# Mixing input projections as three products of rounded parts, their weights split in nine pieces

## What is computed

```python
def token_mix(x, w_in, w_out, ...):
    h = x @ w_in                       # (256, 1024) @ (1024, 2344)
    (nq, kc, vc, ks, vs, kw, vw, gl, u, gq, gk, gv, ga, gr) = jnp.split(h, split_pts, axis=-1)
    gates = jax.nn.sigmoid(gl).reshape(B, S, NSA_HEADS, 3)
    o_a = nsa_mixer(nq, kv(kc), kv(vc), kv(ks), kv(vs), kv(kw), kv(vw), gates, ...)
    o_b = pool_mixer(u, pool_w, pool_scale)
    o_c = gla_mixer(gq, gk, gv, ga, gr, gla_wa2, gla_ba, gla_norm_g)
    return jnp.concatenate([o_a, o_b, o_c], axis=-1) @ w_out
```

## Time and profile before

| what | value |
|---|---|
| time, median of three runs (lowest, highest) | 2362.57 us (2362.32, 2368.52) |
| time of the profiled execution | 2365.88 us |
| its span, first to last instruction | 2364.1 us |
| granted TensorE clock, mean | 0.990 |
| busy: TensorE / weight loads / VectorE / ScalarE / GpSimd | 98% / 81% / 76% / 55% / 7% |
| input projections of mix0, first to last | 201.78 to 263.59 us |

### The profile page before, as it was taken

How to read it: one execution, slowest core, us unless ns; L and a number is a source line. 1 busy time by engine, 2 the same in 40 slices (tenths; PEclk the granted TensorE clock), 3 DMA queues, 4 the chain that set the end, 5 groups by cost and what they waited for, 6 DMA issues and landing times.

```text
span 2364.1 us, 32857 instructions
## 1 busy us (share of the span) xinstructions
PE 2306.4 (98%) x12939; PEld 1907.8 (81%) x12939; DVE 1791.7 (76%) x2006; ACT 1290.6 (55%) x1374; POOL 173.6 (7%) x211
## 2 busy tenths in 40 slices
PE   9999999999999999999999998999999999999997
PEld 7888878878888788889877886678888888888875
DVE  6873468767862678778585568869998989889988
ACT  4432444434432644444544447657777777778774
POOL 1100001000100001000010005400000000000010
PEclk9999999999999999999999998999999999999998
DMA  9766258758655266754135543158999999999994
GB/s 376 268 236 199 90 165 306 265 199 299 244 202 181 108 249 249 268 181 148 72 151 197 190 157 117 73 212 345 382 382 376 379 372 384 385 359 388 382 372 192
DMA packets 116613, 596.88 MB, mean 252 GB/s; under 512 B 29000, under 2 KB 29838, under 8 KB 58638
## 3 DMA queue, kind: packets, MB, share of 16 engines
q1 hardware_dynamic: 95764, 521.10, 57.6%
q0 software_dynamic: 20304, 73.98, 9.2%
q10 hardware_dynamic: 428, 0.15, 0.0%
HBM read 589.38 MB, written 5.78 MB: 252 GB/s over the span
## 4 chain that ended last, share of the span: by engine, by line
PE 90%; DVE 5%; ACT 2%; issue 1%; DMA 1%; ACTq 0%; POOL 0%; DVEq 0%; SPq 0%
PE psum L985 19%; PE psum L986 19%; PE psum L1018 13%; PE psum L1135 6%; PE psum L1564 3%; PE psum L1034 3%; PE psum L1571 3%; PE psum L1152 2%; PE psum L3233 2%; PE psum L978 1%; PE psum L979 1%; PE psum L980 1%; PE psum L2320 1%; PE psum L2323 1%; PE psum L2321 1%; DVE ring_r L1238 1%
## 5 line engine op out<-in xcount | busy, mean ns | idle before, releaser
L1238 DVE TENSOR_TENSOR ring_r<-ring,ring_r 128x2048 fp32r<-128x2048 f32 x286 | 652.3, 2287 | 177.2 <-ACT ring_r L1232 176.9
L1232 ACT CAST ring_r<-ring 128x2048 fp32r<-128x2048 f32 x286 | 546.7, 1913 | 380.0 <-PE psum L1018 206.2
L1238 DVE TENSOR_TENSOR ring_r<-ring,tail_r 128x2048 fp32r<-128x2048 f32 x143 | 327.2, 2288 | 91.6 <-ACT tail_r L1232 91.3
L1232 ACT CAST tail_r<-ring 128x2048 fp32r<-128x2048 f32 x143 | 273.3, 1911 | 141.0 <-PE psum L1018 69.3
L985 PE MATMUL psum<-ring_r,arena_r 128*128 128x512 f32 (+1 forms) x872 | 334.6, 387 | 2.8 <-DVE arena_r L1325 2.8
L986 PE MATMUL psum<-ring_r,arena_r 128*128 128x512 f32 (+1 forms) x872 | 330.9, 382 | 0.0
L985 PE MATMUL psum<-ring_r,xT_r 128*128 128x512 f32 (+1 forms) x576 | 215.7, 380 | 2.9 <-ACT ring_r L1232 2.9
L986 PE MATMUL psum<-ring_r,z_r 128*128 128x512 f32 (+1 forms) x576 | 212.6, 375 | 0.0
L1018 PE MATMUL psum<-ring_r,z_r 128*128 128x512 f32 (+1 forms) x864 | 194.8, 369 | 0.0
L985 PEld LDWEIGHTS psum<-ring_r,arena_r 128*128 128x128 f32 x872 | 164.0, 188 | 34.5 <-DVE arena_r L1325 4.0
L986 PEld LDWEIGHTS psum<-ring_r,arena_r 128*128 128x128 f32 x872 | 164.2, 188 | 30.6
(11 more groups left out here) (582 smaller groups left out, 3737.4 us busy)
## 6 DMA issues: line engine op xcount, KB each, us to landing
ring<-in_expert_halves SPq DMA_DIRECT2D x264, 1024.0 KB, 6.7
ring<-in_dense_halves SPq DMA_DIRECT2D x165, 1024.0 KB, 6.9
arena<-in_ada_w POOLq DMA_DIRECT2D x48, 1024.0 KB, 9.4
ring<-in_mlstm_w_in SPq DMA_DIRECT2D x8, 2048.0 KB, 8.4
ring<-in_mix_in SPq DMA_DIRECT2D x4, 2048.0 KB, 8.7
ring<-in_mix_out SPq DMA_DIRECT2D x4, 2048.0 KB, 7.9
ring<-in_glu_panels SPq DMA_DIRECT2D x4, 2048.0 KB, 9.2
ring<-in_mlstm_w_out SPq DMA_DIRECT2D x3, 2048.0 KB, 13.5
```

The source lines that it names most:

```text
L1232: act.copy(upper[i % UPPERS], place(PN[r.key, i])).then_inc(upper_ready, 1)
L1238: dve.tensor_tensor(low, raw, upper[i % UPPERS], ALU.subtract).then_inc(lower_ready, 1)
```

## The change

Both parts of the input projections are now rounded numbers, as in the feed-forward layers. x is split: `copy_xT_act` writes `xh`, `split_xT_dve` writes the low part to `xT_r` (for tile 0 between the statistics and the centering of tile 1). The weights come in nine pieces of 256 to 280 columns (`IN_PIECES`, ga and gr together are "gr", ks and kw "kskw", vs, vw and gl "vsvw"), each with a semaphore of its own. `in_high_act` copies a piece to its rounded part, `in_low_dve` leaves the low part in place. The parts of gv and gr lie in `ada_w`, and so do later those of vsvw, kskw and kcvc; those of gqk, q01, q23 and u lie in slot 3 and tail. gv and gr are asked for before the preceding feed-forward layer's last three halves are done, and ScalarE and VectorE split them ahead of the layer norm. `features` and `tokens` make 24 calls for 8. w1 is loaded behind kcvc, since slot 3 is taken. gr of tile 1 goes to PSUM bank 7 in place of bank 3; bank 7 is where the second pair of q features goes, which therefore waits for sr. vs, vw and gl tokens are one product of 280 columns into banks 0 and 1, so the attention's first product waits for the gates. The buffers pT and p_sb move into `ada_w` too.

```diff
 
-IN_PANELS = [(1560, 512), (2072, 272), (0, 512), (512, 384), (896, 408), (1304, 256)]
-PANEL_END = ("gv", "gr", "q1", "kcvc", "vwgl", "u")
-Q_PANEL = 2
+IN_PIECES = {"gv": [(1816, 256)], "gr": [(2072, 272)], "gqk": [(1560, 256)], "q01": [(0, 256)], "q23": [(256, 256)],
+             "kskw": [(768, 128), (1024, 128)], "vsvw": [(896, 128), (1152, 128), (1280, 24)], "kcvc": [(512, 256)],
+             "u": [(1304, 256)]}
+IN_WIDTH = {name: sum(n for _, n in cols) for name, cols in IN_PIECES.items()}
+IN_AT = {"gv": 0, "gr": 2048, "gqk": 4224, "q01": 6272, "q23": 8320, "kskw": 0, "u": 2048, "vsvw": 4224, "kcvc": 6464}
+IN_END = {"gv": "gv", "gr": "gr", "gqk": "gqk", "q01": "q0", "q23": "q1", "kskw": "kskw", "vsvw": "vwgl", "kcvc": "kcvc", "u": "u"}
+IN_AFTER = {"kskw": ("gv",), "u": ("gr",), "vsvw": ("q0",), "kcvc": ("q1",)}
 
 ML_INNER, ML_HEADS, ML_CONV, QKV_BLOCK = 2 * D, 4, 4, 4
 ML_HD = ML_INNER // ML_HEADS
@@ -346,7 +350,7 @@
 
...
-            for i in range(len(IN_PANELS)):
-                if i == 3:
-                    PN["mix", l, "w1"] = rg.take(3, dmas=GROUPS, over=mixP.after("cmp0", l))
-                PN["mix", l, "in", i] = rg.take(i % 3, over=mixP.after(PANEL_END[i], l))
+            for name, at in IN_AT.items():
+                places = range(at // HALF, -(-(at + KD * IN_WIDTH[name]) // HALF))
+                PN["mix", l, "in", name] = [mixP.after(e, l) for e in IN_AFTER[name]] if name in IN_AFTER else \
+                    [rg.over[place // 2][place % 2] for place in places]
+            rg.over[0] = [mixP.after("kskw", l), mixP.after("u", l)]
+            rg.over[1] = [mixP.after("vwgl", l), mixP.after("kcvc", l)]
+            rg.over[2] = [mixP.after("kcvc", l), mixP.after("q1", l)]
+            rg.over[3] = [mixP.after("gqk", l), mixP.after("q0", l)]
+            PN["mix", l, "w1"] = rg.take(3, dmas=GROUPS, over=mixP.after("cmp0", l))
...
-            dst = xh[:, t, 4 * b:4 * b + 4, :] if q in FFN_OF else \
+            dst = xh[:, t, 4 * b:4 * b + 4, :] if q in FFN_OF or q in MIX_OF else \
...
-                              xh[:, t, part[0], :], ALU.subtract).then_inc(xl_ready, 1)
+                              xh[:, t, part[0], :], ALU.subtract).then_inc(xl_ready if q in FFN_OF else mix_x_low, 1)
...
+    cv = Carve(ada_w_end - 2 * HALF)
+    pT = cv.take(2, 2 * CHUNK)
+    p_sb = cv.take(2, 2 * CHUNK)
+    cv = Carve(ada_w_end - 2 * HALF, of=arena_r)
+    in_high = {name: cv.take(KD * IN_WIDTH["vsvw"]) for name in ("gr", "gv")}
+    in_high.update(vsvw=in_high["gr"], kskw=in_high["gv"], kcvc=in_high["gv"], gqk=upper[0], q01=upper[1], q23=upper[2], u=upper[2])
...
+    def in_place(name, of=None):
+
+        at, n = IN_AT[name], KD * IN_WIDTH[name]
+        return (ring if of is None else of)[:, :, :].rearrange("p s n -> p (s n)")[:, at:at + n]
+
+    def in_parts(name):
+
+        w = IN_WIDTH[name]
+        return [v[:, 0:KD * w].rearrange("p (k w) -> p k w", w=w) for v in (in_high[name], in_place(name, ring_r))]
+
+    def in_high_act(act, l, name):
+
+        act.wait_ge(in_landed[name], 16 * (l + 1))
+        n = (0, 2)[l]
+        if name in ("gv", "gr"):
+            act.wait_ge(ada_ready, 2 * (n + 1) * NC)
+        elif name in ("gqk", "q01", "q23"):
+            act.wait_ge(halves_used, (n + 1) * FFN_HALVES - 2 + ("gqk", "q01", "q23").index(name))
+        else:
+            act.wait_ge(*mixP.after({"kskw": "gv", "vsvw": "gr", "kcvc": "kskw", "u": "q1"}[name], l))
+        act.copy(in_high[name][:, 0:KD * IN_WIDTH[name]], in_place(name)).then_inc(*inH.inc(name, l))
+
+    def in_low_dve(dve, l, name):
+
+        dve.wait_ge(*inH.after(name, l))
+        dve.tensor_tensor(in_place(name, ring_r), in_place(name), in_high[name][:, 0:KD * IN_WIDTH[name]], ALU.subtract)\
+           .then_inc(*inL.inc(name, l))
+
     def mix_sp(sp, l):
-        for i, (_, n) in enumerate(IN_PANELS):
-            if i == 3:
-                pn = PN["mix", l, "w1"]
-                load_panel(sp, pn, [(slot_of(pn)[d * HD:(d + 1) * HD, :], A["mix_compress"][l]) for d in range(GROUPS)])
-            pn = PN["mix", l, "in", i]
-            load_panel(sp, pn, [(slot_of(pn)[:, 0:KD * n], A[f"mix_in{i}"][l])])
+        for name in ("gv", "gr", "gqk", "q01", "q23", "kskw", "u", "vsvw", "kcvc"):
+            for freed, n in PN["mix", l, "in", name]:
+                sp.wait_ge(freed, n)
+            sp.dma_start(in_place(name), A["mix_in_" + name][l]).then_inc(in_landed[name], 16)
+        pn = PN["mix", l, "w1"]
+        load_panel(sp, pn, [(slot_of(pn)[d * HD:(d + 1) * HD, :], A["mix_compress"][l]) for d in range(GROUPS)])
...
-        return bank(5 - 2 * t)[:, 0:16 + GLA_H * GLA_V]
+        return bank(5 + 2 * t)[:, 0:16 + GLA_H * GLA_V]
 
     def mix_pe(pe, l, q):
-        def features(dst, i, first, m):
-            w = IN_PANELS[i][1]
-            pe.wait_ge(*landed(pn[i]))
+        def features(dst, name, first, m):
+            high, low = in_parts(name)
+            dst = dst.rearrange("p (t n) -> p t n", t=NT)
+            parts = ((xh, high, inH), (xh, low, inL), (None, high, inL))
+            for i, (of, w, ready) in enumerate(parts):
+                pe.wait_ge(*ready.after(name, l))
+                for k in range(KD):
+                    moved = of[:, :, k, :] if of is not None else xT_r[:, k, :].rearrange("p (t n) -> p t n", t=NT)
+                    mm = pe.matmul(dst, w[:, k, first:first + m], moved, start=i == 0 and k == 0, stop=i == 2 and k == KD - 1)
+            return mm
+
+        def tokens(dst, name, t, between=None):
+            high, low = in_parts(name)
+            pe.wait_ge(*inH.after(name, l))
             for k in range(KD):
-                mm = pe.matmul(dst, panel(pn[i], KD, w)[:, k, first:first + m], xT[:, k, :], start=k == 0, stop=k == KD - 1)
-            return mm
-
-        def tokens(dst, i, first, m, t):
-            w = IN_PANELS[i][1]
-            pe.wait_ge(*landed(pn[i]))
+                pe.matmul(dst, xh[:, t, k, :], high[:, k, :], start=k == 0, stop=False)
+            pe.wait_ge(*inL.after(name, l))
             for k in range(KD):
-                mm = pe.matmul(dst, xT[:, k, t * P:(t + 1) * P], panel(pn[i], KD, w)[:, k, first:first + m],
-                               start=k == 0, stop=k == KD - 1)
+                pe.matmul(dst, xh[:, t, k, :], low[:, k, :], start=False, stop=False)
+            if between is not None:
+                between()
+            pe.wait_ge(mix_x_low, 4 * l + 2 * (t + 1))
+            for k in range(KD):
+                mm = pe.matmul(dst, xT_r[:, k, t * P:(t + 1) * P], high[:, k, :], start=False, stop=k == KD - 1)
...
-        tokens(half(4, 0), 0, 256, 256, 0)
-        tokens(decay_gate(0), 1, 0, 272, 0)
-        turn_x(pe, q, 1)
+        tokens(half(4, 0), "gv", 0)
+        tokens(decay_gate(0), "gr", 0, lambda: turn_x(pe, q, 1))
         wait_xT(pe, q)
-        tokens(decay_gate(1), 1, 0, 272, 1).then_inc(*mixP.inc("gr", l))
-        features(half(1, 0), 0, 0, P)
+        tokens(decay_gate(1), "gr", 1).then_inc(*mixP.inc("gr", l))
+        features(half(1, 0), "gqk", 0, P)
         pe.wait_ge(*mixA.after("ga", l))
         for t in range(NT):
             mm = pe.transpose(bank(0)[0:16, t * P:(t + 1) * P], ga[:, t, :], ident)
         mm.then_inc(*mixP.inc("gaT", l))
-        features(half(1, 1), 0, 128, P).then_inc(*mixP.inc("gqk", l))
+        features(half(1, 1), "gqk", P, P).then_inc(*mixP.inc("gqk", l))
         pe.wait_ge(*mixA.after("gaT", l))
         pe.matmul(half(0, 1), gla_wa2[:, l, :], gaT[0:16, :], start=True, stop=True).then_inc(*mixP.inc("pre", l))
-        tokens(half(4, 1), 0, 256, 256, 1).then_inc(*mixP.inc("gv", l))
+        tokens(half(4, 1), "gv", 1).then_inc(*mixP.inc("gv", l))
         for r in range(REP):
-            mm = features(half(6 + r // 2, r % 2), Q_PANEL, r * P, P)
+            if r == 2:
+                pe.wait_ge(*mixA.after("sr", l))
+            mm = features(half(6 + r // 2, r % 2), ("q01", "q23")[r // 2], r % 2 * P, P)
             if r % 2:
...
-        features(half(6, 0), 3, 256, P)
-        features(half(6, 1), 4, 128, P).then_inc(*mixP.inc("kskw", l))
+        features(half(6, 0), "kskw", 0, P)
+        features(half(6, 1), "kskw", P, P).then_inc(*mixP.inc("kskw", l))
...
-        for t in range(NT):
-            mm = tokens(bank(7)[:, t * P:(t + 1) * P], 4, 0, P, t)
-        mm.then_inc(*mixP.inc("vs", l))
         pe.wait_ge(*mixV.after("at", l))
         for t in range(NT):
-            mm = tokens(half(0, t)[:, 0:152], 4, 256, 152, t)
+            mm = tokens(bank(t)[:, 0:IN_WIDTH["vsvw"]], "vsvw", t)
         mm.then_inc(*mixP.inc("vwgl", l))
-        features(half(2, 0), 3, 0, P)
-        features(half(2, 1), 3, 128, P).then_inc(*mixP.inc("kcvc", l))
+        features(half(2, 0), "kcvc", 0, P)
+        features(half(2, 1), "kcvc", P, P).then_inc(*mixP.inc("kcvc", l))
 
 
         pe.wait_ge(*mixV.after("s_blk", l))
+        pe.wait_ge(*mixA.after("gates", l))
...
```

(31 more changed lines are left out.)

27 lines of the change are left out of this document (16 added, 11 removed).

## The result

The changed kernel took 2369.09 us (median of 20 runs, 2364.44 to 2375.73), the kernel before 2365.65 us beside it on the same chips (20 runs, 2360.84 to 2368.67). The ratio is 1.0016, with a 95% interval of 1.0009 to 1.0022: the change costs 2.1 to 5.2 us. That is within the 0.3% that the prediction takes for no change, but on the wrong side of 1 and above the range. The forecast was -2.7 us; about +3.8 us came. The forecast stood on a median of three runs, 2362.57 us; twenty gave 2365.65, so 3.1 of the 9.2 us between 2359.9 and 2369.09 lie in that base.

What follows compares the result with a forecast made beforehand. TensorE, holding 90% of the chain that ended last, was taken as the bound. Two layers' -7.8 us plus +5.1 for the clock gave -2.7, so 2362.57 became 2359.9 us, range 2353 to 2366.

Steps and rivals of the forecast that it cites:

- The price of a product: Input projections on TensorE: 0.12 us per 256-column product, so 24 take 2.88 us instead of 3.45.
- rival 2: Products cheaper than 0.12 us, paced by columns alone at 107 ns: 2352.5 us; chance 0.04.
- Norm of tile 0: Before the projections: VectorE subtracts gr ahead of the layer norm, so TensorE gets x of tile 0 later, +0.8 us.
- First tokens: 201.78 to 214.43 us: TensorE stalls 2.4 us for VectorE's low part of x; the stretch still nets -0.3 us.
- the wait for sr: Before the third q feature: TensorE stalls 3.7 us for silu, behind the kskw copy on ScalarE; stretch nets +1.4 us.
- rival 3: Transfers late because pieces share the queues, so kskw lands after 9 us instead of 5: 2376.7 us; chance 0.08.
- 239.65 to 263.59: Stretch of kskw and kcvc features and value tokens: cheaper products, weight loads covered, -3.9 us per layer.
- u: Two u groups: up to -1.3 us, but VectorE's p holds TensorE back, so -0.2 us per layer.
- the sum of a layer: Mixing layer's terms: 0.8 - 0.3 - 1.7 + 1.4 - 3.9 - 0.2 = -3.9 us; two layers -7.8 us.
- The clock: TensorE's clock falls to half at both long stalls and one of two short ones: 3 x 1.7 = +5.1 us.
- Rival 1: The clock holds at 1.00 despite the stalls in the mixing layers: 2354.8 us; chance 0.23.
- Rival 4: The splitting moves nothing, gains end in waits for the kskw copy and VectorE: within 2 us of 2362.6; chance 0.10.

Runs made afterwards that it cites:

- e2: Changed kernel with ScalarE's rounding of kskw moved behind the silu of the output gates; 2357.60 us.
- e4: Kernel before, first mix_out panel held back to the end of the kcvc products, a second, unused 2 MB mix_out load right behind it; 2371.78 us.
- e9: Changed kernel with kskw rounding behind silu, first tile's products needing only rounded x put first, second mix_out panel released after u; 2350.37 us.
- e10: Changed kernel, kskw rounding behind silu, first-tile products reordered, both mix_out panels later, first panel's rounding and subtraction behind third and fourth scores' softmax; 2349.94 us.

## Why the prediction was wrong

**The bound.** TensorE was the bound, and every new idle stretch reached the end, as the first part had it.

**The price of a product** was right: 24 in 2.88 us. So rival 2, with 107 to 109 ns, falls.

**Norm of tile 0**, +0.8 in each layer: measured 0.65, and at most 0.27 in layer 1. Right in layer 0, too high in layer 1.

**First tokens and the wait for sr.** Idle of 2.4 and 3.7 us forecast, 2.13 and 3.20 to 3.39 measured, at the lines named, ended by the engines named. kskw landed after 4.7 us and u, issued with it, after 6.9: in turn and not shared, so rival 3 falls. e2 showed that the sr wait was the order of ScalarE's queue and nothing more.

**239.65 to 263.59**, -3.9: measured -3.84, in both layers. Right. No low part of vsvw or kcvc was waited for.

**u**, -0.2: too small. Without the new idle on issue and with the falls taken off at what they cost here, compression to output projection is 0.5 and 0.8 us shorter. So VectorE held back less of it than I took.

**The step that failed** is the sum of a layer behind the projections: it holds the -0.2 of u and puts everything else there at nothing, without a reason. The prediction priced the landing of the projection pieces, and never the two mix_out panels, whose release is tied to the projections that the change reorders. It moves both to the start of compression, where the queues had been idle. This brought 2.76 + 0.69 us in layer 0 and 2.87 where 0.48 stood in layer 1, **+5.8 us**, with no term. e4 shows it alone: +5.9 us, of it 4.5 more idle on issue than before, and one fall of the clock.

**The clock**, +5.1, was right in kind and mis-sized: six falls came in the profiled execution and not three, **+8.9**. The price of 1.7 us was near the 1.4 to 1.6 measured, in part by luck: it was the middle of a range for low stretches of 6.8 us, and these are 3.41 long. Both long silu waits brought one, as forecast; of the two 2.13 us waits one did; one came behind the issue idle in layer 1. Two (294 and 810 us) came with only 0.36 us of idle beside them, behind 32 products of 16 columns; no run settled what set them off. Rival 1, the held clock, falls. What spoke for it, the wait ahead of 11.26 us without a fall, was the chance of one execution: the changed kernel waits 2.67 us at the same place, and there the clock fell.

In sum, the two layers gave +4.7 in the profiled execution: 5.8 of issue and 8.9 of clock, and -10.0 from the terms that stood at -7.8. Of these 2.2 us, some 0.7 is the norm, 1.3 the four waits and 0.9 u, and 0.7 goes the other way, for the most part in the projections up to the transposes of kd. Rival 4 (nothing moves) falls: the products did get 3.8 us cheaper where nothing waited. e9 and e10 show where the gain went: with the two forecast waits and the panels' cost taken away or made small, the same products give -15 us on the kernel before. That goes past -7.8, since that sum held the two waits as costs.

## What to carry to other kernels

When a change reorders work that frees buffers, list every transfer that the old order released, the ones that the change does not name too, and ask beside which work they now run. A stretch with very many small instructions can be slowed by transfers with which it shares no data, since its own instructions come in over the DMA queues too; the sign is idle put down to issue beside a DMA share near 1. An in-order engine that splits weights should do it behind whatever TensorE will ask of that engine next, and a wait of over 2 us on a busy TensorE is to be priced with a chance of about two in three (21 of 33 here) of another 1.5 us for the clock.
